# Retention: the query and key products of chunks 1 to 7 in one matmul over both parts of u and one over the upper part

## The chip, the cores and the metric

One core of a Trainium2 chip runs the whole program in one launch. The metric is the device time of one execution in microseconds (us). Engines are written as the profile writes them: PE is TensorE's matmuls, PEld its weight loads, DVE is VectorE, ACT is ScalarE, POOL is GpSimd, SP is the engine that issues the weight loads from HBM.

## The reference, cut to what matters

The reference is a transformer of six layers over 256 rows of 1024 numbers. Each layer has a mixer and an MLP; the first and the fourth mixer are retention:

```python
def retention(u, positions, w_in, decay_logit, w_out):
    q, k, v, g = jnp.split(u @ w_in, [qk, 2 * qk, 2 * qk + vd], axis=-1)
    q = rotary(split_heads(q, RET_HEADS), positions) * (RET_QK_DIM ** -0.5)
    k = rotary(split_heads(k, RET_HEADS), positions)
    ...
    o = bidirectional_scan(q, k, v, lg(0), lg(1))
    o = merge_heads(rmsnorm(o)) * jax.nn.silu(g)
    return o @ w_out
```

Queries and keys are 4 heads of 256 columns each, so `u @ w_in` has 2048 columns for q and k, 2048 for v and 2048 for g. The rotation multiplies both halves of a head by a cosine table, and the swapped halves by a sine table.

## The kernel before

Everything is float32. A product is made exact enough by splitting each operand into an upper part, rounded to a short form, and a lower part, the rest; three of the four products are summed. For u the two parts lie in `U[p, k, t, l, n]`: k is one of 8 blocks of the inner dimension, t the row half, l the part (0 upper, 1 lower), n one of 128 rows. For the weights the parts lie in `whi` and `wlo`.

**Weights.** They come in 1 MB chunks, in a fixed order. SP loads chunk i into one of 4 raw buffers. ScalarE (`hi_half`, line 1464) copies each half of it to `whi`; VectorE (`lo_half`, line 2049) subtracts to get `wlo`. `whi` and `wlo` hold two chunks each. So the upper part of half x of chunk i+2 is made only once TensorE is done with half x of chunk i: `hi_half` waits for `USED[i, x]`. VectorE's subtraction waits for that copy.

**Queries and keys.** In a retention stage, chunks 0 to 7 hold the columns of q (0 to 3) and k (4 to 7), one head to a chunk. Chunk 0 goes through `gemm_up_first` into banks 0 and 1 of the accumulator memory. Chunks 1 to 7 go through `gemm_b`: for each half (128 weight columns) and each of the 8 blocks, three matmuls of 256 columns, all summed in the same half bank, 48 matmuls a chunk. They use the banks 4 + n % 4, so four chunks in turn; chunk n waits that ScalarE has copied chunk n-4 (`QKCP`), from chunk 5 on.

**What the other engines do with them.** Each engine runs its instructions in the order in which they are written. In a retention stage, where n counts the stage's chunks and "hi" and "lo" are the two splitting steps:

- ScalarE (`act_ret`): hi of chunks 0 to 2, `raw(0)`, then for n from 2 to 8: hi of chunk n+1, `raw(n-1)`. `raw` copies a chunk's sums to `raw_q`.
- VectorE (`dve_ret`): lo of chunks 0 to 3, `tables`, `rotate(0)`, then for n from 3 to 9: lo of chunk n+1, `rotate(n-2)`. `rotate` makes four operations, lines 2276 to 2282. For chunk 0 alone it first adds the two sums (line 2274), since `gemm_up_first` leaves them apart.
- After chunk 7, TensorE goes on with the columns of v and g through `gemm_a` (line 680).

Of the kernel before, what the change touches and what calls it, by code (L numbers as in the profile page):

```python
# [11 lines left out]
ALU = mybir.AluOpType  # L12
ACT = mybir.ActivationFunctionType
# [62 lines left out]
def program(nc, d, out):  # L76
    with ExitStack() as ctx:
# [3 lines left out]
        def sem(name):  # L81
            return ctx.enter_context(nc.semaphore(name))
# [20 lines left out]
        def bank(b, n=1):  # L103
            return PS[:, b * 512:(b + n) * 512]
# [410 lines left out]
        DEC = Event(sem("s_ret_decay_exp"), heads4)  # L515
        eight = [(S, n) for S in RETS for n in range(8)]
        QKCP = Event(sem("s_ret_qk_copied"), eight)
        ROT = Event(sem("s_ret_rotated"), eight)
        RV = Event(sem("s_ret_v"), [(S, n, tt) for S in RETS for n in (0, 1) for tt in range(2)])
        RG = Event(sem("s_ret_gate"), [(S, n, tt) for S in RETS for n in (2, 3) for tt in range(2)])  # L520
# [153 lines left out]
        def pe_program(e):  # L674
# [111 lines left out]
            def gemm_b(i, b, free=(), mid=None):  # L786

                for s in range(2):
# [10 lines left out]
                            mm = e.matmul(o, a[:, k, :], U[:, k, :, part, :], start=(k == 0 and n == 0), stop=(k == 7 and n == 2))  # L799
                    mm.then_inc(USED.tick((i, s)), 1)  # L800

            def gemm_up(i, b, free):

                for ev in free:
                    e.wait_ge(*ev)
                for s in range(2):
                    e.wait_ge(*lo_cut(i, s))
                    w_h, w_l = split_half(whi, i, s), split_half(wlo, i, s)
                    o = bank(b + s).rearrange("p (t l n) -> p t l n", t=2, l=2)
                    for k in range(8):  # L810
                        if k:
                            e.matmul(o[:, :, 0, :], w_l[:, k - 1, :], U[:, k - 1, :, 0, :], start=False, stop=False)  # L812
                        if k == 7:
                            e.matmul(o[:, :, 0, :], w_l[:, k, :], U[:, k, :, 0, :], start=False, stop=False)  # L814
                        mm = e.matmul(o, w_h[:, k, :], U[:, k, :, :, :], start=(k == 0), stop=(k == 7))  # L815
                    mm.then_inc(USED.tick((i, s)), 1)
# [87 lines left out]
            def pe_ret(S):  # L904
                p, c0 = PR, first[S]
                gemm_up_first(c0, 0, (S, "in"))
                for n in range(1, 8):
                    gemm_b(c0 + n, 4 + n % 4, free=[] if n < 5 else [QKCP[S, n - 4]])
                    if n == 1:
                        rows_of_r(S, p.dg, 3)  # L910

                def scores(hh):
                    e.wait_ge(*ROT[S, 4 + hh])
                    e.wait_ge(*(RPT[S, hh - 1] if hh else ROT[S, 7]))
                    for s in range(2):
                        for k in range(2):
                            mm = e.matmul(PS[:, 4 * 512 + s * 256:4 * 512 + s * 256 + 256],  # L917
                                          p.kT[:, 2 * hh + k, s * 128:(s + 1) * 128], p.qT[:, 2 * hh + k, :],
                                          start=(k == 0), stop=(k == 1))
                    mm.then_inc(RSC.tick((S, hh)), 1)  # L920

                def values(hh):
                    e.wait_ge(*RPT[S, hh])
                    for tt in range(2):
                        if hh:
                            e.wait_ge(*RON[S, hh - 1, tt])
                        if tt == 0:
                            e.wait_ge(*RV[S, hh // 2, 1])
                        for s in range(2):
                            mm = e.matmul(bank(5 + tt), p.PT[:, hh % 2, s * 256 + tt * 128:s * 256 + tt * 128 + 128],  # L930
                                          p.v[:, s, hh * 512:(hh + 1) * 512], start=(s == 0), stop=(s == 1))
                        mm.then_inc(RAV.tick((S, hh, tt)), 1)

                def turn(hh, jj):
                    b = o_bank[hh % 2][jj]
                    if hh == 0:
                        if jj:
                            e.wait_ge(*RPT[S, 3])
                    elif hh == 1:
                        e.wait_ge(*RON[S, 3, jj])  # L940
                    else:
                        e.wait_ge(*ROL[S, hh - 2, jj])
                    for kk in range(2):
                        for tt in range(2):
                            if jj == 0 and kk == 0:
                                e.wait_ge(*RGG[S, hh, tt])
                            og = p.o[hh][tt].rearrange("p a n -> p (a n)")
                            o = b * 512 + kk * 256 + tt * 128
                            k = 2 * jj + kk
                            tr = e.transpose(PS[:, o:o + 128], og[:, k * 128:(k + 1) * 128], ident[:, :])  # L950
                    tr.then_inc(RTO.tick((S, hh, jj)), 1)

                def o_ap(hh):
                    return lambda k, tt: (p.oH[hh][:, k, tt, :], p.oL[hh][:, k, tt, :])

                def v_0(c):
                    pass

                def v_1(c):
                    if c == 1:  # L960
                        scores(0)
                    if c == 2:
                        values(0)

                def g_0(c):
                    (scores, values)[c % 2](1 + c // 2)

                def g_1(c):
                    if c == 0:
                        scores(3)  # L970
                    if c == 1:
                        values(3)
                    if c >= 2:
                        turn(0, c - 2)

                for n, after in enumerate((v_0, v_1, g_0, g_1)):
                    free = (([ROT[S, 0]], [ROPE[S]]),
                            ([RV[S, 0, 0]], [RV[S, 0, 1]]),
                            ([RV[S, 1, 0]], [RV[S, 1, 1]]),
                            ([RG[S, 2, 0]], [RG[S, 2, 1]]))[n]  # L980
                    gemm_a((S, n), c0 + 8 + 4 * n, 8, u_ap, (0, 2), free=free, after=after, entry=lambda: None)
                for hh in range(3):
                    gemm_a((S, "y"), c0 + 24 + 2 * hh, 4, o_ap(hh), (0, 2), fresh=lambda k, tt: [ROL[S, hh, k // 2]],
                           free=([RG[S, 3, 0]], [RG[S, 3, 1]]), begins=(hh == 0), ends=False,
                           after=lambda c: turn(hh + 1, c), entry=(lambda: None) if hh == 0 else None)
                gemm_last(S, o_ap(3), lambda k, tt: [ROL[S, 3, k // 2]])
# [466 lines left out]
        def act_program(e):  # L1453
# [118 lines left out]
            def act_ret(S):  # L1572
                p, c0 = PR, first[S]

                def raw(n):
                    e.wait_ge(*USED[c0 + n, 1])
                    if n >= 2:
                        e.wait_ge(*ROT[S, n - 2])
                    if n == 0:

                        a = bank(0, 2).rearrange("p (s t l n) -> p s t l n", s=2, t=2, l=2)
                        ins = e.activation(p.raw_q[:, 0, :, :].rearrange("p s (t n) -> p s t n", t=2), a[:, :, :, 1, :], ACT.Copy)
                    else:
                        ins = e.activation(p.raw_q[:, n % 2, :, :], bank(4 + n % 4).rearrange("p (a n) -> p a n", a=2), ACT.Copy)
                    ins.then_inc(QKCP.tick((S, n)), 1)

                def log_decay():
                    e.wait_ge(*s_ret_par["decay"][RETN[S]])
# [451 lines left out]
        def dve_program(e):  # L2040
# [19 lines left out]
            def own(ins):  # L2060
                ins.then_inc(dve_own.tick(), 1)

            def settle():

                e.wait_ge(*dve_own.now())
# [160 lines left out]
            def dve_ret(S):  # L2226
# [40 lines left out]
                def rotate(n):  # L2267
                    s = n % 2
                    dst = (p.qT if n < 4 else p.kT)[:, 2 * (n % 4):2 * (n % 4) + 2, :]
                    e.wait_ge(*QKCP[S, n])  # L2270
                    if n == 0:
                        a = bank(0, 2).rearrange("p (s t l n) -> p s t l n", s=2, t=2, l=2)
                        x = p.raw_q[:, 0, :, :].rearrange("p s (t n) -> p s t n", t=2)
                        own(e.tensor_tensor(x, a[:, :, :, 0, :], x, ALU.add))
                        settle()
                    own(e.tensor_tensor(dst, p.raw_q[:, s, :, :], cosb, ALU.mult))
                    if n:
                        e.wait_ge(*ROT[S, n - 1])
                    own(e.tensor_tensor(p.tb, p.raw_q[:, s, :, :], sinb, ALU.mult))
                    settle()  # L2280
                    e.tensor_tensor(dst[:, 0, :], dst[:, 0, :], p.tb[:, 1, :], ALU.subtract)
                    e.tensor_tensor(dst[:, 1, :], dst[:, 1, :], p.tb[:, 0, :], ALU.add).then_inc(ROT.tick((S, n)), 1)
# [972 lines left out]
```

## Time and profile before

| | us |
|---|---|
| three runs, median | 2210.44 |
| three runs, lowest and highest | 2209.98 and 2210.93 |
| the profiled execution, first to last instruction | 2208.3 |
| PE busy | 2174.9 |
| DVE busy | 1481.4 |
| ACT busy | 1196.9 |

Busy time of an engine is the time in which it had at least one instruction in flight. Matmuls overlap each other, so the time that one costs is read from the distance between the starts of two, not from its duration. The two retention stages begin at 0 and at about 1020 us of the profile.

### The profile page before, as it was taken

How to read it: one execution, taken by the hardware profiler on the slowest of the kernel's cores; microseconds unless marked ns; L12 is line 12 of the kernel's file. 1: busy time of each engine (PE TensorE's matmuls, PEld its weight loads, DVE VectorE, ACT ScalarE, POOL GpSimd, SP SyncE). 2: the span in 40 equal slices, each digit the busy share in tenths (PEclk: the TensorE clock that was granted, in tenths of full speed). 3: DMA queues.
4: the chain of work that ended last, by engine and by line, in shares of the span. 5: the costliest groups of instructions: out<-in, count | busy, mean ns of one | idle time of the engine just before them, and what ended most of it. 6: DMA issues, size and time to landing. Idle time of an engine off the chain costs nothing.

```text
span 2208.3 us, 29721 instructions
## 1 busy us (share of the span) xinstructions
PE 2174.9 (98%) x11776; PEld 1838.2 (83%) x11776; DVE 1481.4 (67%) x2057; ACT 1196.9 (54%) x1814; POOL 217.1 (10%) x228
## 2 busy tenths in 40 slices
PE   9999999999999999999999999999999999999999
PEld 9878888997888878888877888787888888877887
DVE  7645755897556767657745755687655699685655
ACT  5555544756445645455555544566544566475443
POOL 0000100472000011000000200002000100051000
PEclk9999999999999999999999999999999999999999
DMA  8544656524655435555544655551655566513653
GB/s 267 185 134 153 203 191 191 164 76 121 210 190 164 171 115 193 189 191 172 184 148 157 176 189 193 180 172 58 205 191 191 176 174 190 172 39 103 200 189 119
DMA packets 201817, 368.95 MB, mean 167 GB/s; under 512 B 6991, under 2 KB 142543, under 8 KB 201680
## 3 DMA queue, kind: packets, MB, share of 16 engines
q1 hardware_dynamic: 198064, 358.70, 49.7%
q0 software_dynamic: 3616, 8.35, 2.3%
q8 instruction: 95, 1.56, 0.3%
q14 instruction: 42, 0.34, 0.0%
HBM read 365.97 MB, written 1.05 MB: 166 GB/s over the span
## 4 chain that ended last, share of the span: by engine, by line
PE 90%; DVE 6%; ACT 2%; POOL 1%; issue 1%; DMA 0%; DVEq 0%; ACTq 0%; POOLq 0%
PE PS L680 48%; PE PS L815 14%; PE PS L812 6%; PE PS L799 6%; PE PS L850 2%; PE PS L1009 2%; PE PS L930 1%; DVE wlo L2049 1%; PE PS L857 1%; PE PS L1100 1%; PE PS L814 1%; POOL wlo L2977 1%; ACT whi L1464 1%; PE PS L1364 1%; PE PS L917 1%
## 5 line engine op out<-in xcount | busy, mean ns | idle before, releaser
L2049 DVE TENSOR_TENSOR wlo<-raw,whi 128x1024 fp32r<-128x1024 f32 x658 | 790.7, 1229 | 181.2 <-ACT whi L1464 180.4
L1464 ACT ACTIVATE whi<-raw 128x1024 fp32r<-128x1024 f32 x680 | 699.8, 1054 | 363.9 <-PE PS L680 309.0
L680 PE MATMUL PS<-whi,U 128*128 128x512 f32 x1728 | 483.8, 396 | 6.5 <-DVE U L2086 1.4
L815 PE MATMUL PS<-U,whi 128*128 128x512 f32 x1344 | 474.4, 397 | 0.0
L680 PEld LDWEIGHTS PS<-whi,U 128*128 128x128 f32 x1728 | 321.6, 188 | 80.8 <-issue 13.5
L812 PE MATMUL PS<-U,wlo 128*128 128x256 f32 x1176 | 330.0, 281 | 0.0
L815 PEld LDWEIGHTS PS<-U,whi 128*128 128x128 f32 x1344 | 247.1, 188 | 48.6
L2173 DVE TENSOR_TENSOR AR<-PS,AR 128x512 f32<-128x512 f32 x96 | 66.3, 691 | 309.3 <-ACT AR L1550 309.3
L680 PE MATMUL PS<-wlo,U 128*128 128x512 f32 x864 | 267.4, 391 | 0.0
L1550 ACT ACTIVATE AR<-PS 128x512 f32<-128x512 f32 x96 | 57.6, 600 | 368.6 <-PE PS L815 358.6
L680 PE MATMUL PS<-whi,fH 128*128 128x512 f32 x824 | 255.8, 392 | 0.9 <-DVE fL L2311 0.9
L680 PE MATMUL PS<-whi,fL 128*128 128x512 f32 x824 | 253.8, 389 | 0.0
L680 PE MATMUL PS<-wlo,fH 128*128 128x512 f32 x824 | 253.8, 389 | 0.0
L812 PEld LDWEIGHTS PS<-U,wlo 128*128 128x128 f32 x1176 | 222.1, 189 | 6.5
L680 PEld LDWEIGHTS PS<-wlo,U 128*128 128x128 f32 x864 | 162.5, 188 | 34.8
L2977 POOL TENSOR_TENSOR wlo<-raw,whi 128x1024 fp32r<-128x1024 f32 x22 | 52.2, 2390 | 1339.4 <-ACT whi L1464 870.3
L680 PEld LDWEIGHTS PS<-wlo,fH 128*128 128x128 f32 x824 | 154.7, 188 | 32.8
L680 PEld LDWEIGHTS PS<-whi,fL 128*128 128x128 f32 x824 | 154.7, 188 | 32.2
L680 PEld LDWEIGHTS PS<-whi,fH 128*128 128x128 f32 x824 | 153.2, 188 | 30.7 <-DVE wlo L2049 1.3
L799 PE MATMUL PS<-U,whi 128*128 128x256 f32 x768 | 139.1, 284 | 0.0
L799 PEld LDWEIGHTS PS<-U,whi 128*128 128x128 f32 x768 | 119.7, 192 | 0.4 <-DVE wlo L2049 0.3
L799 PE MATMUL PS<-U,wlo 128*128 128x256 f32 x384 | 108.6, 283 | 0.0
(342 smaller groups left out, 2356.1 us busy)
## 6 DMA issues: line engine op xcount, KB each, us to landing
raw<-in_mlp_w_up SPq DMA_DIRECT2D x64, 1024.0 KB, 5.6
raw<-in_mlp_w_down SPq DMA_DIRECT2D x64, 1024.0 KB, 5.0
raw<-in_ret_w_in SPq DMA_DIRECT2D x48, 1024.0 KB, 5.2
raw<-in_m_w_up SPq DMA_DIRECT2D x32, 1024.0 KB, 5.5
raw<-in_m_w_down SPq DMA_DIRECT2D x32, 1024.0 KB, 4.9
raw<-in_kv_w SPq DMA_DIRECT2D x24, 1024.0 KB, 5.2
raw<-in_ret_w_out SPq DMA_DIRECT2D x16, 1024.0 KB, 4.9
raw<-in_gla_w_in SPq DMA_DIRECT2D x12, 1024.0 KB, 5.1
```

The source lines that it names most:

```text
L680: mm = e.matmul(bank(b + nb), a, w[:, nb * 512:(nb + 1) * 512], start=(begins and n < 2), stop=(ends and n >= 4))
L799: mm = e.matmul(o, a[:, k, :], U[:, k, :, part, :], start=(k == 0 and n == 0), stop=(k == 7 and n == 2))
L812: e.matmul(o[:, :, 0, :], w_l[:, k - 1, :], U[:, k - 1, :, 0, :], start=False, stop=False)
L814: e.matmul(o[:, :, 0, :], w_l[:, k, :], U[:, k, :, 0, :], start=False, stop=False)
L815: mm = e.matmul(o, w_h[:, k, :], U[:, k, :, :, :], start=(k == 0), stop=(k == 7))
L850: e.matmul(o, w[:, k, :], U[:, k, tt, :, :], start=(tt == 0 and k == 0), stop=False, skip_group_check=True)
L1009: e.matmul(PS[:, b * 512 + o:b * 512 + o + 256], p.diag[:, tap_turn[c, jt] % 32, :], p.hc[:, c, jt:jt + 256], start=(jt == 0), stop=(jt == ...
L1464: e.activation(split_half(whi, i, x), raw_halves(i)[x], ACT.Copy).then_inc(HI.tick((i, x)), 1)
L1550: e.activation(m_t[f % 2].rearrange("p (s n) -> p s n", s=4), a[:, :, 1, :], ACT.Copy).then_inc(MT.tick((S, f)), 1)
L2049: e.tensor_tensor(split_half(wlo, i, x), raw_halves(i)[x], split_half(whi, i, x).bitcast(F32), ALU.subtract).then_inc(LO.tick((i, x)), 1)
L2173: e.tensor_tensor(x.rearrange("p (s n) -> p s n", s=4), a[:, :, 0, :], m_t[f % 2].rearrange("p (s n) -> p s n", s=4), ALU.add).then_inc(MX ...
L2977: e.tensor_tensor(split_half(wlo, i, x), a, split_half(whi, i, x).bitcast(F32), ALU.subtract).then_inc(LO_SEAM.tick((i, x)), 1)
```

## The change

`gemm_heads` takes the place of `gemm_b` for chunks 1 to 7 of both retention stages. For each half, 8 matmuls of 512 columns multiply the upper weights with both parts of u, into a bank whose columns are kept apart by part; then 8 matmuls of 256 columns add the product of the lower weights with the upper part of u. One half takes a bank, a chunk two: odd chunks use banks 4 and 5, even ones 6 and 7. From chunk 3 on, chunk n waits that VectorE has added the two sums of chunk n-2 (`QKADD`). TensorE waits for `HI` before a half and for the lower weights in its middle. ScalarE copies the sums of the lower part to `raw_q` and VectorE adds those of the upper part to it before it rotates, as both did before for chunk 0 alone.

```diff
+        QKADD = Event(sem("s_ret_qk_added"), eight)
+        def qk_bank(n):
+            return 0 if n == 0 else 4 if n % 2 else 6
...
+            def gemm_heads(i, b, free):
+                for ev in free:
+                    e.wait_ge(*ev)
+                for s in range(2):
+                    e.wait_ge(*HI[i, s])
+                    w_h, w_l = split_half(whi, i, s), split_half(wlo, i, s)
+                    o = bank(b + s).rearrange("p (t l n) -> p t l n", t=2, l=2)
+                    for k in range(8):
+                        e.matmul(o, w_h[:, k, :], U[:, k, :, :, :], start=(k == 0), stop=False, skip_group_check=True)
+                    e.wait_ge(*lo_cut(i, s))
+                    for k in range(8):
+                        mm = e.matmul(o[:, :, 0, :], w_l[:, k, :], U[:, k, :, 0, :], start=False, stop=(k == 7),
+                                      skip_group_check=True)
+                    mm.then_inc(USED.tick((i, s)), 1)
...
-                    gemm_b(c0 + n, 4 + n % 4, free=[] if n < 5 else [QKCP[S, n - 4]])
+                    gemm_heads(c0 + n, qk_bank(n), [QKADD[S, n - 2]] if n >= 3 else [])
...
-                    if n == 0:
-                        a = bank(0, 2).rearrange("p (s t l n) -> p s t l n", s=2, t=2, l=2)
-                        ins = e.activation(p.raw_q[:, 0, :, :].rearrange("p s (t n) -> p s t n", t=2), a[:, :, :, 1, :], ACT.Copy)
-                    else:
-                        ins = e.activation(p.raw_q[:, n % 2, :, :], bank(4 + n % 4).rearrange("p (a n) -> p a n", a=2), ACT.Copy)
-                    ins.then_inc(QKCP.tick((S, n)), 1)
+                    a = bank(qk_bank(n), 2).rearrange("p (s t l n) -> p s t l n", s=2, t=2, l=2)
+                    e.activation(p.raw_q[:, n % 2, :, :].rearrange("p s (t n) -> p s t n", t=2), a[:, :, :, 1, :],
+                                 ACT.Copy).then_inc(QKCP.tick((S, n)), 1)
...
-                    if n == 0:
-                        a = bank(0, 2).rearrange("p (s t l n) -> p s t l n", s=2, t=2, l=2)
-                        x = p.raw_q[:, 0, :, :].rearrange("p s (t n) -> p s t n", t=2)
-                        own(e.tensor_tensor(x, a[:, :, :, 0, :], x, ALU.add))
-                        settle()
+                    a = bank(qk_bank(n), 2).rearrange("p (s t l n) -> p s t l n", s=2, t=2, l=2)
+                    x = p.raw_q[:, s, :, :].rearrange("p s (t n) -> p s t n", t=2)
+                    e.tensor_tensor(x, a[:, :, :, 0, :], x, ALU.add).then_inc(QKADD.tick((S, n)), 1)
+                    e.wait_ge(*QKADD[S, n])
```

## Rows read from the trace of the kernel before

**Rows 1.** The page: busy time of TensorE, and the chain that ended last.
```profile
PE 2174.9 (98%) x11776; PEld 1838.2 (83%) x11776; DVE 1481.4 (67%) x2057; ACT 1196.9 (54%) x1814; POOL 217.1 (10%) x228
...
PE 90%; DVE 6%; ACT 2%; POOL 1%; issue 1%; DMA 0%; DVEq 0%; ACTq 0%; POOLq 0%
```

**Rows 2.** TensorE's waits (total, times, longest): the longest of all.
```profile
PE PS L1364 <- DVE AR L2873: 3.6, 5, 1.9
```

**Rows 3.** Timeline of TensorE, first stage (start, length, instructions): edges of chunks 1, 2, 8.
```profile
20.90 0.40 PE L799 MATMUL PS<-U,whi 128*128 128x256 f32 x2
...
26.66 0.60 PE L886 MATMUL PS<-AR,ones 128*128 128x128 f32 x4
27.02 0.48 PE L799 MATMUL PS<-U,whi 128*128 128x256 f32 x2
...
61.66 0.63 PE L680 MATMUL PS<-whi,U 128*128 128x512 f32 x2
...
62.59 1.07 PE L680 MATMUL PS<-whi,U 128*128 128x512 f32 x4
...
63.95 1.07 PE L680 MATMUL PS<-whi,U 128*128 128x512 f32 x4
```

**Rows 4.** Timeline of TensorE in an MLP, where 512 and 256 columns alternate.
```profile
234.17 0.40 PE L815 MATMUL PS<-U,whi 128*128 128x512 f32 x1
...
236.65 0.28 PE L814 MATMUL PS<-U,wlo 128*128 128x256 f32 x1
```

**Rows 5.** Timeline of ScalarE, first stage: the copies to `whi`, with waits.
```profile
32.96 2.01 ACT L1464 ACTIVATE whi<-raw 128x1024 fp32r<-128x1024 f32 x2 [0.50 <-DMA raw<-in_ret_w_in]
...
61.86 1.06 ACT L1464 ACTIVATE whi<-raw 128x1024 fp32r<-128x1024 f32 x1 [1.76 <-PE PS L799]
```

**Rows 6.** Timeline of VectorE, first stage.
```profile
34.12 0.69 DVE L2274 TENSOR_TENSOR AR<-PS,AR 128x512 f32<-128x512 f32 x1
34.84 0.69 DVE L2276 TENSOR_TENSOR AR<-AR 128x512 f32<-128x512 f32 x1
...
36.85 2.35 DVE L2049 TENSOR_TENSOR wlo<-raw,whi 128x1024 fp32r<-128x1024 f32 x2
39.12 0.69 DVE L2276 TENSOR_TENSOR AR<-AR 128x512 f32<-128x512 f32 x1
...
43.39 0.68 DVE L2276 TENSOR_TENSOR AR<-AR 128x512 f32<-128x512 f32 x1
...
62.96 1.23 DVE L2049 TENSOR_TENSOR wlo<-raw,whi 128x1024 fp32r<-128x1024 f32 x1 [1.40 <-ACT whi L1464]
64.10 0.69 DVE L2276 TENSOR_TENSOR AR<-AR 128x512 f32<-128x512 f32 x1
```

**Rows 7.** The chain in order of time: from VectorE's end to TensorE's start.
```profile
84.11 0.14 issue
```

**Rows 8.** Timeline of TensorE at that place.
```profile
84.24 0.70 PE L680 MATMUL PS<-whi,U 128*128 128x512 f32 x2 [0.63 <-DVE AR L2287]
```

**Rows 9.** Timeline of VectorE, second stage: lo of chunk 4, second half.
```profile
1044.91 1.23 DVE L2049 TENSOR_TENSOR wlo<-raw,whi 128x1024 fp32r<-128x1024 f32 x1 [0.33 <-ACT whi L1464]
```

**Rows 10.** Stretches: busy of PE, PEld, DVE, ACT, POOL; then granted clock, DMA.
```profile
506.00:507.00 1.00, 0.61 (x2) 0.55 (x3) 0.63 (x4) 0.89 (x3) 0.00 (x0) 0.57 0.00 0
...
508.00:509.00 1.00, 1.00 (x4) 0.80 (x3) 1.00 (x3) 0.40 (x1) 0.00 (x0) 0.50 0.00 0
509.00:510.00 1.00, 1.00 (x4) 0.73 (x3) 0.96 (x2) 0.97 (x3) 0.00 (x0) 0.72 0.00 0
```

**Rows 11.** Timeline of TensorE at that place.
```profile
506.39 1.19 PE L680 MATMUL PS<-whi,U 128*128 128x512 f32 x2 [1.11 <-DVE U L2502]
...
510.24 1.08 PE L680 MATMUL PS<-whi,U 128*128 128x512 f32 x4
```

**Rows 12.** Timeline of TensorE at another fall (1943), and the same transposes later.
```profile
1942.48 1.07 PE L1364 MATMUL PS<-AR 64*128 64x128 f32 x12 [1.86 <-DVE AR L2873]
1943.48 2.82 PE L1379 MATMUL PS<-ident,xn 128*128 128x128 f32 x12
...
1987.69 1.53 PE L1379 MATMUL PS<-ident,xn 128*128 128x128 f32 x12
```

## The prediction

> **What bounds the kernel now.** I read the page first: TensorE is busy for 98% of the span and holds 90% of the chain that ended last [rows 1]. Then its waits: the longest single one of the whole program is 1.9 us [rows 2], and none lies in the chunks that the change touches. So a microsecond of matmuls saved is a microsecond gained, and every new wait of TensorE is paid in full. Then the timelines of the three engines in the first retention stage. TensorE takes chunk 1 from 20.90 to 26.66 us, which is 48 matmuls at a pitch of 0.120, and runs on without a gap until chunk 8 starts at 61.66 [rows 3]. ScalarE and VectorE work inside that: what they do per chunk is hidden, but the order in which they do it decides what TensorE will wait for once it depends on one of them.
>
> **The matmuls.** Before, a half chunk is 24 x 0.120 = 2.88 us. After, it is 8 of 512 columns and 8 of 256. From 62.59 to 63.95 six matmuls of 512 columns start, so 0.227 each [rows 3], and 256 columns keep 0.120: 8 x 0.227 + 8 x 0.120 = 2.78 us, a gain of 0.10. The nearest row of the same mixture is that of the MLP: seven pairs in 236.65 - 234.17 = 2.48 us [rows 4], so 8 pairs in 2.83, a gain of 0.05. I take 0.10, since the new order groups the widths; the MLP's row is the lower bound and 0.11 the upper. There are 2 stages x 7 chunks x 2 halves = 28: a gain of 2.8 us (1.4 to 3.1). The columns are as many as before, and only the instructions are a third fewer.
>
> The Trainium skill, "TensorE: Matmul & The Clock Gate", section "Wait — 56ns, not 53.3ns?", gives a matmul in a row its columns at 2.4 GHz and about 2.5 ns. By that a half chunk would gain 8 x 2.5 ns = 0.02 us, the whole 0.6. The rows here show 13 ns over the columns' time both at 256 and at 512, so they disagree with it, and the sum goes by them.
>
> **What goes beside other work.** VectorE gets 14 additions (7 chunks, 2 stages); the one of chunk 0 takes 0.69 us and the next operation starts 0.72 after it [rows 6]. Where VectorE runs unbroken, from one rotation to the next is 43.39 - 39.12 = 4.3 us [rows 6]; with 0.72 it is 5.0, under the 5.56 of a new chunk. So VectorE as an amount of work still fits, and after chunk 7 its waits for ScalarE take the addition up. ScalarE's copy keeps its size. The additional waits of TensorE inside a half (`HI`, then lo) are for things done a chunk earlier: nothing.
>
> **The new wait is not hidden.** Before, four banks in turn let TensorE run four chunks ahead of ScalarE's copies. Now two pairs of banks turn, and chunk n+1 waits for the addition of chunk n-1. That addition stands in VectorE's order behind lo of chunk n+2 (the loop makes lo of chunk n+1, then `rotate(n-2)`). Lo of chunk n+2 waits for hi of chunk n+2, and the hi of its second half waits for `USED[n, 1]`, the last matmul of chunk n, since `whi` holds two chunks. So TensorE can't start chunk n+1 when chunk n ends: it waits for a full round through ScalarE and VectorE. That isn't a deadlock, as each step waits for an earlier one, but it is a stall ahead of each of the chunks 3, 4, 5, 6 and 7, in both stages: ten.
>
> Its price, step by step, from the moment at which the next matmul would have started:
> - to the start of hi: 61.86 - 61.66 = 0.20 [rows 3, 5]
> - hi to lo: 62.96 - 61.86 = 1.10 [rows 5, 6]
> - lo to the next operation of VectorE: 64.10 - 62.96 = 1.14 [rows 6]; this next one is now the addition
> - the addition: 0.69 [rows 6]
> - VectorE's end to TensorE's start: 0.14 [rows 7]
> - the first matmuls after a wait run slower: two take 0.70 [rows 8] where two take 0.63 without a wait [rows 3], 0.07.
>
> Sum 3.34 us (I allow 3.2 to 3.5). What is queued behind TensorE's wait is the whole stream of matmuls, and with it `USED`, and so the hi of the next chunks: the round can't overlap the next one.
>
> The first of the ten is longer, in the first stage. There hi of chunk 4 starts at 32.96, when its weights land [rows 5], and VectorE is behind: `rotate(0)` from 34.12, lo of chunk 4 from 36.85, next operation at 39.12 [rows 6]. None of these moves. So chunk 3 can start at 39.12 + 0.69 + 0.14 = 39.95. TensorE gets there at 20.90 + 5.56 + 0.44 (the small matmuls between, 26.66 to 27.02, and the slower one behind them, 0.08 [rows 3]) + 5.56 = 32.46. Stall 7.5, with the slow start 7.6. In the second stage lo of chunk 4 waits for ScalarE in its second half [rows 9], so that stage's first stall is an ordinary one.
>
> Sum: 9 x 3.34 + 7.6 = 37.7 us lost, 2.8 gained: +34.9.
>
> **The clock.** No row shows TensorE idle for 3.34 us amid full-width matmuls, so what its clock does then is bounded from both sides. Rows near it: at 506 us, after 1.11 us idle behind matmuls of one row, the granted clock was 0.57, then 0.50, that is 1.2 GHz in place of 2.4, and it came back within 509 to 510 [rows 10]. Ten matmuls of 512 columns took 510.24 - 506.39 = 3.85 us where ten at 0.227 take 2.27 [rows 11]: 1.6 lost. The fall around 1943 followed the 1.86 us of idle time, and 12 transposes took 2.82 us [rows 12] where the same 12 take 1.53 at full clock. The new stalls are nearly twice as long as the longest of these, but what surrounds them is denser. Lower end: nothing. Upper end: ten falls at 1.6, 16 us. I take eight falls at 1.5, 12 us, because the stall is longer than each idle time after which the clock fell here. In the touched chunks this is paid in full, since the round starts from the last matmul of a chunk.
>
> The Trainium skill's same page, section "HAM oscillation — how this bites in real kernels", tells of a kernel in which each wait between bursts put the clock back to half, and the next burst started slow, every time. By that rule all ten stalls would cost a fall.
>
> **The total.** The profiled execution's span is 2208.3, the median of the runs 2210.4, so 2.1 us lie around the span; the sum is of differences within it and leaves them as they are. 2210.4 + 34.9 + 12 = 2257.3; I predict 2257, 2.1% slower.
>
> **Rivals.**
> - The stalls come but the clock stays at 2.4 GHz, or falls only after the long one: 2210.4 + 34.9 = 2245, to 2247. For it: over the chunks TensorE stays busy for 5.56 of each 8.9 us. Against it: rows 10 and 12, with less idle time. 20%.
> - Every stall costs a fall and the matmuls gain only the lower bound: 9 x 3.45 + 7.6 = 38.7, 38.7 + 16 - 1.4 = 53 us, 2264. 15%.
> - Not slower: the round is not closed. If the addition of chunk n-1 is done before chunk n ends, TensorE never waits and only the matmuls' gain stays: 2210.4 - 2.8 = 2207.6 (2207.3 to 2209). This would decide if VectorE were to reach `rotate(n-1)` before TensorE ends chunk n, so if lo of chunk n+2 didn't need chunk n's buffer. Rows 6 speak against it: 64.10 follows the lo that waited for chunk 7's end. 3%.
> - The stalls are there but shorter, since part of the round overlaps the end of the matmuls, or because only the first stage is hit: some 20 us, 2230. 4%.
> - The forecast: ten stalls and most of them with a fall, 2250 to 2262. 58%.
>
> **How the numbers follow.** Differences under 0.2% (4.4 us) can't be told from no change here. The rival without stalls is -2.8 us, inside of that. So slower has 0.96, same 0.03, faster 0.01. The range for 8 in 10 goes from the case without falls at its lower bounds (9 x 3.25 + 7.5 - 3.1 = 33.7, 2244, less 2 for the sum's error) to the case with all of them: 2242 to 2265.
>
> **What would show it.** In the changed kernel's trace TensorE should wait for the addition of VectorE ten times, near 7.5 us once and near 3.3 nine times, at the starts of chunks 3 to 7. The chunks should start some 8.9 us apart, more where the clock fell; within a chunk at full clock the half should take 2.78. The granted clock should show 0.5 for some 3 us after most stalls. VectorE's addition should start about 1.1 us after a second-half lo. I would be wrong on the main step if TensorE shows no waits in these chunks, and on the clock if the row of granted clock stays at 1.00 in both stages.

## The result, and the profile after

The changed kernel takes 2261.03 us (median of four runs, 2259.41 to 2261.79) where the kernel before takes 2210.21: a ratio of 1.0229, 95% interval 1.0217 to 1.0241. The forecast was 2257, with a range of 2242 to 2265. The profiled execution spans 2260.0 us, 51.7 more than that of before.

The page of the changed kernel, and TensorE's longest waits (total, times, longest):

```profile
PE 2190.0 (97%) x11552; PEld 1838.0 (81%) x11552; DVE 1491.7 (66%) x2071; ACT 1196.5 (53%) x1814; POOL 217.0 (10%) x228
...
PE 88%; DVE 7%; ACT 2%; DMA 1%; POOL 1%; issue 1%; SPq 0%; DVEq 0%; ACTq 0%
```
```profile
PE PS L817 <- DVE AR L2291: 35.0, 10, 8.0
```

The first line answers to rows 1: 224 matmuls fewer, yet more busy time, because part of them ran at half clock. The second answers to rows 2. L817 is the first matmul of `gemm_heads`, L2291 the addition in `rotate`. Ten waits, five in each stage, one of them 8.0 us and the nine others 3.0.

The timeline of TensorE in the first stage (start, length, instructions; in brackets the idle time ahead and what ended it), all of chunks 1 to 3, the start of chunk 4, chunk 7, and the start of chunk 8:

```profile
22.06 2.00 PE L817 MATMUL PS<-U,whi 128*128 128x512 f32 x8
23.90 1.12 PE L820 MATMUL PS<-U,wlo 128*128 128x256 f32 x8
24.86 2.00 PE L817 MATMUL PS<-U,whi 128*128 128x512 f32 x8
26.70 1.11 PE L820 MATMUL PS<-U,wlo 128*128 128x256 f32 x8
27.65 0.60 PE L908 MATMUL PS<-AR,ones 128*128 128x128 f32 x4
28.01 2.10 PE L817 MATMUL PS<-U,whi 128*128 128x512 f32 x8
29.95 1.11 PE L820 MATMUL PS<-U,wlo 128*128 128x256 f32 x8
30.89 2.00 PE L817 MATMUL PS<-U,whi 128*128 128x512 f32 x8
32.73 1.11 PE L820 MATMUL PS<-U,wlo 128*128 128x256 f32 x8
41.82 3.78 PE L817 MATMUL PS<-U,whi 128*128 128x512 f32 x8 [7.98 <-DVE AR L2291]
45.40 1.62 PE L820 MATMUL PS<-U,wlo 128*128 128x256 f32 x8
46.86 1.99 PE L817 MATMUL PS<-U,whi 128*128 128x512 f32 x8
48.69 1.11 PE L820 MATMUL PS<-U,wlo 128*128 128x256 f32 x8
52.81 3.33 PE L817 MATMUL PS<-U,whi 128*128 128x512 f32 x8 [3.01 <-DVE AR L2291]
...
84.03 3.69 PE L817 MATMUL PS<-U,whi 128*128 128x512 f32 x8 [3.00 <-DVE AR L2291]
87.56 1.11 PE L820 MATMUL PS<-U,wlo 128*128 128x256 f32 x8
88.51 2.00 PE L817 MATMUL PS<-U,whi 128*128 128x512 f32 x8
90.35 1.11 PE L820 MATMUL PS<-U,wlo 128*128 128x256 f32 x8
91.30 0.63 PE L686 MATMUL PS<-whi,U 128*128 128x512 f32 x2
```

This answers to rows 3. A half chunk at full clock goes from 22.06 to 24.86, 2.80 us. Behind a stall the first half takes 4.48 (84.03 to 88.51), and the second one 2.79 again: the half that follows the idle stretch is slow, and only that one.

From the start of chunk 1 to that of chunk 8, the first stage took 61.66 - 20.90 = 40.76 us before and takes 91.30 - 22.06 = 69.24 now; the second stage took 40.76 and takes 63.42. That is 28.5 and 22.7 us more, 51.1 of the 51.7 together. The rest (a first stage that begins 1.2 us later, and 0.6 us less in all that follows) is of the size by which two executions of one kernel differ.

One round, in the chain that ended last (start, length, what), in the second stage:

```profile
1083.59 0.96 PE PS L820 x8
1084.55 0.02 issue
1084.58 1.06 ACT whi L1486
1085.64 0.02 issue
1085.66 1.22 DVE wlo L2067
1086.89 0.61 DVE AR L2291
1087.50 0.04 issue
1087.54 3.69 PE PS L817 x8
```

In this list a piece ends where the next one takes over, so the addition stands with less than its own 0.68 us. It can be read from top to bottom as the prediction's list: the last matmuls of a chunk, the copy to `whi` that waited for them, the subtraction, the addition, and only then the next chunk. This answers to rows 5, 6 and 7.

### The profile page after: what moved, and what is told of

Read it like the earlier page. It is cut to its first block, busy times and chain, and to the rows that moved or that the text cites. A ratio compares the mean times of both kernels' runs of the same rounds, so it can differ in the third digit from the quotient of the medians.

```text
span 2260.0 us, 29291 instructions
## 1 busy us (share of the span) xinstructions
PE 2190.0 (97%) x11552; PEld 1838.0 (81%) x11552; DVE 1491.7 (66%) x2071; ACT 1196.5 (53%) x1814; POOL 217.0 (10%) x228
## 4 chain that ended last, share of the span: by engine, by line
PE 88%; DVE 7%; ACT 2%; DMA 1%; POOL 1%; issue 1%; SPq 0%; DVEq 0%; ACTq 0%
PE PS L686 47%; PE PS L837 14%; PE PS L834 6%; PE PS L817 3%; PE PS L805 3%; PE PS L872 2%; PE PS L1031 2%; DVE wlo L2067 2%; PE PS L952 1%; DMA raw<-in_ret_w_in 1%; PE PS L820 1%; PE PS L879 1%; ACT whi L1486 1%; PE PS L1122 1%; PE PS L836 1%
## 5 line engine op out<-in xcount | busy, mean ns | idle before, releaser
L837 PE MATMUL PS<-U,whi 128*128 128x512 f32 x1344 | 474.5, 397 | 0.0
L834 PE MATMUL PS<-U,wlo 128*128 128x256 f32 x1176 | 330.0, 281 | 0.0
L837 PEld LDWEIGHTS PS<-U,whi 128*128 128x128 f32 x1344 | 247.1, 188 | 48.5
L817 PE MATMUL PS<-U,whi 128*128 128x512 f32 x224 | 72.1, 476 | 35.0 <-DVE AR L2291 35.0
L817 PEld LDWEIGHTS PS<-U,whi 128*128 128x128 f32 x224 | 49.7, 232 | 47.3 <-DVE AR L2291 37.1
L2104 DVE SCALAR_TENSOR_TENSOR U<-PS,gT,U 128x128 fp32r<-128x128 f32 x192 | 52.5, 342 | 36.6 <-ACT U L1518 36.6
```

The costliest lines, as they stand in the source:

```text
L2104: ins = e.scalar_tensor_tensor(U[:, k, tt, 1, :], PS[:, o:o + 128], gT[:, S + 1, k:k + 1], U[:, k, tt, 0, :].bitcast(F32), ALU.mult, ALU.s ...
```

## Experiments

**Only the place of the addition: e1_rotate_earlier.**

```diff
                 for n in range(3, 10):
+                    rotate(n - 2)
                     lo_of(c0 + n, 1)
-                    rotate(n - 2)
```

> The changed kernel, but VectorE rotates chunk n-2 (and so adds its two sums) one place earlier in its order: ahead of lo of chunk n+1 in place of behind it. Banks, waits and matmuls as in the changed kernel. My theory (TensorE's wait closes a round through hi and lo of a chunk whose buffer is still in use): the addition is then done some 3 us into the next chunk, so eight of the ten waits vanish; only chunk 3 still waits, some 5 us in the first stage and 1 us in the second, with one fall of the clock: 2210.2 - 2.3 + 6.3 + 2 = 2216 us. Rival (the 14 additions make VectorE too slow, or two pairs of banks are too few in any order): above 2240 us.

Measured: 2217.95 us, ratio 1.0034 (1.0021 to 1.0047). Of ten waits two are left, and they are those that the swap can't remove:

```profile
PE PS L817 <- DVE AR L2291: 5.7, 2, 5.2
```

One is of 5.2 us in the first stage, one of 0.5 in the second; in the first the clock fell, around the second it stayed at 1.00. The time is 2 us above the 2216 that was expected. With the same banks, the same 14 additions and the same matmuls, 43 of the 51 us are gone. So neither VectorE's work nor the number of banks alone makes the stalls, but that the addition stands behind a subtraction which waits for the chunk that has just ended.

**Only a third pair of banks: e2_three_pairs.** VectorE's order is that of the changed kernel.

```diff
-            return 0 if n == 0 else 4 if n % 2 else 6
+            return (0, 4, 6, 0, 4, 6, 2, 4)[n]
...
-                    gemm_heads(c0 + n, qk_bank(n), [QKADD[S, n - 2]] if n >= 3 else [])
+                    qk_free = {3: [QKADD[S, 0]], 4: [QKADD[S, 1]], 5: [QKADD[S, 2]], 6: [ROPE[S]], 7: [QKADD[S, 4]]}
+                    gemm_heads(c0 + n, qk_bank(n), qk_free.get(n, []))
...
-                    free = (([ROT[S, 0]], [ROPE[S]]),
+                    free = (([QKADD[S, 3]], [QKADD[S, 6]]),
```

> The changed kernel with VectorE's order left as it is, but a third pair of banks: chunks 1 to 7 use the pairs 4, 6, 0, 4, 6, 2, 4, so that chunk n waits for the addition of chunk n-3 (chunk 6 for the tables, which read bank 3), and the first product behind chunk 7 waits for the additions of chunks 3 and 6. My theory: with one chunk more of distance the round through hi and lo isn't closed. Left are a wait of chunk 3 in the first stage (2.5 to 3.5 us, perhaps one fall of the clock, 1.7) and about 0.6 us ahead of the second rows of chunk 8 in each stage: 2212 to 2215 us. Rival (VectorE is too slow as an amount of work): the waits move by one chunk and come back, above 2230 us.

Measured: 2214.48 us, ratio 1.0018 (1.0008 to 1.0027), with ten runs from 2212.1 to 2217.7. The profiled execution is one of the quick ones (span 2210.4). In it TensorE waits at the places that were named, and for less:

```profile
34.76 2.11 PE L817 MATMUL PS<-U,whi 128*128 128x512 f32 x8 [1.82 <-DVE AR L2292]
```
```profile
66.06 0.70 PE L686 MATMUL PS<-whi,U 128*128 128x512 f32 x2 [0.36 <-DVE AR L2292]
```

The second kind comes once in each stage. The order that closes the round at a distance of two chunks doesn't at a distance of three. Around the first wait the clock stays at 1.00 (stretches of 2 us: length, busy time of PE, PEld, DVE, ACT, POOL, then granted clock and DMA), and the half behind it takes 37.65 - 34.76 = 2.89 us:

```profile
32.00:34.00 2.00, 0.94 (x8) 0.73 (x7) 1.98 (x4) 1.47 (x3) 0.00 (x0) 1.00 1.10 349
34.00:36.00 2.00, 1.24 (x5) 1.05 (x6) 1.95 (x3) 0.89 (x1) 0.00 (x0) 1.00 1.10 348
```

So 1.8 us of idle time between full chunks cost no fall here. What makes the longer runs of this kernel longer isn't in the one trace. Their mean granted clock hints at a fall: 0.995 over the whole of the two longest (2217.4 and 2217.7 us), 0.998 in the two quickest. A longer first wait with a fall behind it would fit, as in e1; it isn't shown.

**Is it the distance of two, or who releases? e8_before_two_banks.** The kernel before the change, with two banks in turn; the release is ScalarE's copy.

```diff
-                    gemm_b(c0 + n, 4 + n % 4, free=[] if n < 5 else [QKCP[S, n - 4]])
+                    gemm_b(c0 + n, 4 + n % 2, free=[] if n < 3 else [QKCP[S, n - 2]])
...
-                        ins = e.activation(p.raw_q[:, n % 2, :, :], bank(4 + n % 4).rearrange("p (a n) -> p a n", a=2), ACT.Copy)
+                        ins = e.activation(p.raw_q[:, n % 2, :, :], bank(4 + n % 2).rearrange("p (a n) -> p a n", a=2), ACT.Copy)
```

> The kernel before the change with two banks in turn in place of four: chunk n waits for ScalarE's copy of chunk n-2. It tells whether a distance of two chunks is itself too short, or only the place of the releasing operation in VectorE's order. My theory: ScalarE's copy of chunk n-2 is done some 2 us into chunk n-1, well ahead, so there is no wait: 2210.5 us, within 0.1%. Rival (a distance of two is too short with any releaser): waits at chunks 3 to 7, 2230 us or more.

Measured: 2211.27 us, ratio 1.0003 (0.9994 to 1.0012), and in chunks 1 to 7 no wait of TensorE for a bank. One wait is there, ahead of chunk 2 of the first stage, for the lower weights, which no bank decides; ScalarE starts on the weights of chunk 2 at 26.12 us in this execution and at 24.02 in that of before, so they came later:

```profile
28.50 0.50 PE L799 MATMUL PS<-U,whi 128*128 128x256 f32 x2 [0.69 <-DVE wlo L2049]
```

The second stage takes 40.76 us from chunk 1 to chunk 8, as before. The kernel before had twice the banks that it needed. Two are enough if the release comes early in the next chunk; with the same distance, it is the release's place that decides.

**Is the slow first half the clock? e3_fill_stalls.** Matmuls of no use ahead of each wait; they add nothing to the result. The trace records each of them as two.

```diff
+                    if n >= 3:
+                        for _ in range(32 if (S, n) == (RET0, 3) else 12):
+                            e.matmul(PS[:, 2 * 512:2 * 512 + 128], ones[:, :], ones[:, :], start=True, stop=True)
                     gemm_heads(c0 + n, qk_bank(n), [QKADD[S, n - 2]] if n >= 3 else [])
```

> The changed kernel with matmuls of no use ahead of each of the ten waits: 12 of 128 columns in float32 (about 2.7 us at full clock; 32 ahead of the first one, about 7 us), into a bank that nobody uses there, so that TensorE doesn't idle. The waits themselves, their releasers and all useful work stay. My theory (each idle stretch of 3.2 us costs a fall of the clock, 1.7 us): granted clock 1.00 in both stages, the time falls by 9 x 1.7 + 2.2 = 17 us to 2244 us. Rival (the slow first half chunk comes from something else, such as both parts of u being read, or the banks): the time stays at 2261 us or rises.

Measured: 2245.05 us, ratio 1.0163 (1.0146 to 1.0180), 16.0 us less than the changed kernel, where 17 were expected. The stretches, in the same columns, of the changed kernel around one stall:

```profile
1084.00:1085.00 1.00, 0.54 (x5) 0.33 (x3) 0.17 (x1) 0.42 (x1) 0.00 (x0) 1.00 0.00 0
1085.00:1086.00 1.00, 0.00 (x0) 0.00 (x0) 0.34 (x1) 1.00 (x2) 0.00 (x0) 1.00 0.00 0
1086.00:1087.00 1.00, 0.00 (x0) 0.00 (x0) 1.00 (x2) 0.12 (x1) 0.00 (x0) 1.00 0.00 0
1087.00:1088.00 1.00, 0.46 (x1) 0.46 (x2) 0.97 (x2) 0.00 (x0) 0.00 (x0) 0.80 0.10 16
1088.00:1089.00 1.00, 1.00 (x4) 0.72 (x4) 0.97 (x3) 0.00 (x0) 0.00 (x0) 0.50 0.82 131
...
1090.00:1091.00 1.00, 1.00 (x4) 0.81 (x3) 0.00 (x0) 0.00 (x0) 0.00 (x0) 0.50 1.00 414
1091.00:1092.00 1.00, 1.00 (x9) 0.94 (x9) 0.00 (x0) 0.00 (x0) 0.00 (x0) 1.00 0.24 94
```

and with the stalls filled, the timeline of TensorE around one of them and a stretch over one:

```profile
46.73 2.84 PE L932 MATMUL PS<-ones 128*128 128x128 f32 x24
49.90 2.12 PE L817 MATMUL PS<-U,whi 128*128 128x512 f32 x8 [0.33 <-DVE AR L2294]
51.85 1.11 PE L820 MATMUL PS<-U,wlo 128*128 128x256 f32 x8
```
```profile
49.00:52.00 3.00, 2.67 (x16) 2.13 (x15) 2.90 (x6) 0.00 (x0) 0.00 (x0) 1.00 0.56 128
```

The wait still ends at the same point of the round (46.73 + 3.17 = 49.90), but the first half behind it takes 2.90 us (49.90 to 52.80), not 4.48, and the clock stays at 1.00, as it does in all of both stages. So the slow half is the clock at 1.2 GHz, and it comes from idling, not from the matmuls' form or the banks. In the stall shown TensorE had just gone back to work, at 1087.54, when the clock fell: a mean of 0.80 over 1087 to 1088 puts the fall at 1087.6, and the three stretches ahead have 1.00. The rule of the Trainium skill that the prediction named ("TensorE: Matmul & The Clock Gate", section "HAM oscillation — how this bites in real kernels"), half clock behind every wait between bursts, is what this trace shows at ten stalls of ten; the shorter waits of 1.8 us in e2 and 0.5 us in e1 were not followed by a fall.

**The matmuls' form, with the stalls: e4_old_matmul_form.**

```diff
-                    for k in range(8):
-                        e.matmul(o, w_h[:, k, :], U[:, k, :, :, :], start=(k == 0), stop=False, skip_group_check=True)
                     e.wait_ge(*lo_cut(i, s))
                     for k in range(8):
+                        e.matmul(o[:, :, 0, :], w_h[:, k, :], U[:, k, :, 0, :], start=(k == 0), stop=False, skip_group_check=True)
+                        e.matmul(o[:, :, 1, :], w_h[:, k, :], U[:, k, :, 1, :], start=False, stop=(k == 7), skip_group_check=True)
                         mm = e.matmul(o[:, :, 0, :], w_l[:, k, :], U[:, k, :, 0, :], start=False, stop=(k == 7),
```

> The changed kernel with its banks, its waits on the addition and its stalls, but each half chunk again by 24 matmuls of 256 columns (the upper weights times the upper part of u, times the lower part, the lower weights times the upper part), the two sums still apart. It prices the matmuls' form by itself. My theory: at full clock a half takes 2.88 in place of 2.80 us, at half clock both are bound by their columns, so 1.5 to 2.3 us more than the changed kernel: 2263 us, with the same ten waits. Rival (the form with 512 columns is itself what makes the stages slow): back towards 2215 us.

Measured: 2261.18 us, ratio 1.0234 (1.0219 to 1.0250). The form is not what makes the stages slow, so the rival is out. But my number for its price isn't seen either: 0.2 us more than the changed kernel, where 1.5 to 2.3 were expected. The second stage, from chunk 1 to chunk 8, is 63.47 us, against 63.42. In the first stage the first wait hides it: it is 5.9 us long here and 8.0 in the changed kernel's execution, since it depends on when the weights of the first chunks land:

```profile
PE PS L818 <- DVE AR L2291: 33.0, 10, 5.9
```

In the second stage the clock hides it. Its five slow halves take 21.29 us together here and 22.01 in the changed kernel, so they give back 0.72 of the 0.77 us that the nine quick ones cost more (0.086 each, from e7 and e5 below). At half clock the form costs nothing that can be seen: the matmuls start every 0.21 us, which is 256 columns at 1.2 GHz. And the fall came earlier against TensorE's return: in the second of these stalls the clock was at 0.50 already 0.2 us ahead of it, where the changed kernel's fell just behind it, so that less of the low clock met work. The form had to be measured without stalls.

**Both repairs: e5_order_and_pairs.**

```diff
-            return 0 if n == 0 else 4 if n % 2 else 6
+            return (0, 4, 6)[n % 3]
...
-                    gemm_heads(c0 + n, qk_bank(n), [QKADD[S, n - 2]] if n >= 3 else [])
+                    gemm_heads(c0 + n, qk_bank(n), [QKADD[S, n - 3]] if n >= 3 else [])
...
-                    free = (([ROT[S, 0]], [ROPE[S]]),
+                    free = (([QKADD[S, 6]], [ROPE[S]]),
...
-                lo_of(c0, 3)
+                lo_of(c0, 2)
                 tables()
                 rotate(0)
-                for n in range(3, 10):
+                for n in range(2, 9):
                     lo_of(c0 + n, 1)
-                    rotate(n - 2)
+                    rotate(n - 1)
+                lo_of(c0 + 9, 1)
```

> The changed kernel with both repairs: a third pair of banks (chunks 1 to 7 use the pairs 4, 6, 0 in turn, so that chunk n waits for the addition of chunk n-3), and VectorE rotates each chunk directly behind lo of the chunk two further on (lo of chunks 0 to 2, tables, rotation 0, lo 3, rotation 1, lo 4, rotation 2 and so on). My theory: TensorE never waits in chunks 3 to 7, nor ahead of chunk 8, the clock stays at 1.00, and what is left is the matmuls' gain, 28 x 0.08 = 2.3 us: 2208 us, ratio 0.999. Rival (the change has another cost that the stalls hid, such as ScalarE and VectorE now reading banks beside TensorE's writes): 2211 us or more without any wait.

Measured: 2207.47 us, ratio 0.9988 (0.9979 to 0.9997): faster than the kernel before, by 2.6 us. The stretches of the two stages:

```profile
20.00:62.00 42.00, 42.00 (x249) 37.20 (x248) 38.02 (x58) 23.95 (x32) 0.95 (x2) 1.00 0.89 294
1030.00:1072.00 42.00, 42.00 (x246) 37.11 (x245) 38.06 (x57) 20.63 (x26) 0.00 (x0) 1.00 0.60 193
```

TensorE is busy in all of both, at full clock, and never waits for the addition, while VectorE is busy for 38 of 42 us: the cover of the additions is nearly used up, but it holds. From chunk 1 to chunk 8 each stage takes 39.55 us (21.94 to 61.49 in the first), 1.21 less than before.

**The form without stalls: e7_old_form_repaired.** The kernel of e5, with the matmuls of e4.

> The kernel with both repairs (e5_order_and_pairs), but each half chunk by 24 matmuls of 256 columns, as before the change; the two sums stay apart. It prices the matmuls' form without stalls. My theory: 2.88 in place of 2.80 us a half, 2.3 us more than e5_order_and_pairs: 2210.2 us. Rival (the gain is only in how the records are modelled, not in time): the same time as e5_order_and_pairs.

Measured: 2211.20 us, ratio 1.0004 (0.9995 to 1.0013), 3.7 us more than e5. Each stage takes 40.76 us from chunk 1 to chunk 8, to the hundredth the number of the kernel before. So at full clock the form is worth 1.21 us a stage, 2.4 in all, and it is the whole of the gain that the two stages show. The other 1.3 of the 3.7 us lies outside of them and stays open; it is of the size by which two executions of one kernel differ. The additions and the third pair cost nothing in these stages.

**Grouped or alternating: e6_widths_alternating.** The kernel of e5, but in each half the two widths take turns (the last two of 256 columns stand together), and the lower weights are waited for at the head:

```diff
-                    for k in range(8):
-                        e.matmul(o, w_h[:, k, :], U[:, k, :, :, :], start=(k == 0), stop=False, skip_group_check=True)
                     e.wait_ge(*lo_cut(i, s))
                     for k in range(8):
-                        mm = e.matmul(o[:, :, 0, :], w_l[:, k, :], U[:, k, :, 0, :], start=False, stop=(k == 7),
-                                      skip_group_check=True)
+                        if k:
+                            e.matmul(o[:, :, 0, :], w_l[:, k - 1, :], U[:, k - 1, :, 0, :], start=False, stop=False)
+                        if k == 7:
+                            e.matmul(o[:, :, 0, :], w_l[:, k, :], U[:, k, :, 0, :], start=False, stop=False)
+                        mm = e.matmul(o, w_h[:, k, :], U[:, k, :, :, :], start=(k == 0), stop=(k == 7))
```

> The kernel with both repairs (e5_order_and_pairs), but in each half the matmuls of 512 and 256 columns alternate, as the MLP's do, and TensorE waits for the lower weights ahead of the half. It tells what the grouping by width is worth. By the MLP's rows a half takes 2.82 in place of 2.80 us: 28 x 0.02 = 0.6 us more than e5_order_and_pairs, which the times can hardly tell; the trace should show the pitch. If the wait for the lower weights matters, TensorE waits at chunk 3 of the first stage.

Measured: 2208.09 us, ratio 0.9991 (0.9982 to 1.0000); its interval and that of e5 overlap. In the trace the second stage takes 39.82 us from chunk 1 to 8, 0.27 more than e5's. The first takes 40.64 us, and part of that is a wait for the lower weights, at chunk 2 and not at chunk 3 as expected:

```profile
29.02 0.47 PE L822 MATMUL PS<-U,whi 128*128 128x512 f32 x1 [0.38 <-DVE wlo L2068]
```

## Why the prediction was right

**What bounds the kernel.** Right. The waits are paid in full, and so is the gain: 2.4 us less in the two stages gave 2.6 in the time (e5 against the kernel before).

**The matmuls.** 2.78 us a half were forecast, 2.80 came, so the gain is 2.4 in place of 2.8 us, within its bounds. The distance of 0.227 between matmuls of 512 columns was read where the moving operand is a weight; here it is (23.90 - 22.06) / 8 = 0.230. The figure that the prediction worked out from the Trainium skill ("TensorE: Matmul & The Clock Gate", section "Wait — 56ns, not 53.3ns?"), 0.6 us for the whole, doesn't hold here: e7 and e5 differ by 2.4 in the trace.

**What goes beside other work.** Right: VectorE is busy for 10.3 us more (1481.4 to 1491.7), 14 x 0.72 being 10.1, and e5 has every addition and not one wait of TensorE for it.

**The new wait.** Right in kind, place and number: ten waits for L2291, ahead of chunks 3 to 7 of both stages. Where the next chunk would have started at 1084.38 (1083.43 and 0.95 for the last eight), it starts at 1087.54, so 3.16 us, and the first matmuls behind a wait cost 0.11 more (2.12 behind the waits of e3, at full clock, where 2.00 is usual). That is 3.27 for the 3.34 of the sum. The small difference is in the last step: from the start of the addition to TensorE's start it took 0.73 us, and I had added 0.69 and 0.14. A duration in the profile and a release overlap, which the two rows taken from different places couldn't show. The first stall is 41.82 - 33.68 = 8.1 us where 7.5 were expected. ScalarE starts on the weights of chunk 4 when they land, here at 34.94 us and not at 32.96:

```profile
34.94 2.00 ACT L1486 ACTIVATE whi<-raw 128x1024 fp32r<-128x1024 f32 x2 [0.52 <-DMA raw<-in_ret_w_in]
```

So chunk 3 starts 1.9 us later than expected, while TensorE got there only 1.2 us later. In e4 that start was at 32.38 and the idle time 5.9 us, so much of this stall is chance. The sum of all, nine times 3.27 and once 8.25, is 37.7, as forecast to the tenth; that is luck in part, since 0.6 us too much in the nine and 0.6 too little in the first cancel.

**The clock.** The range was right and the value low. All ten stalls brought a fall, where I took eight, a value between the bounds that no row decided. Behind an ordinary stall the first half took 4.31 to 4.48 us in place of 2.79; without the slow start that is 1.4 to 1.6 us, the size that rows 11 and 12 gave. Behind the long one it was 2.1. Together 15.9 us, in place of 12; e3, without the falls, is 16.0 us shorter. That is the term that was mis-sized, and with 0.4 us for the matmuls it makes up the whole difference: 2257.3 + 3.9 + 0.4 = 2261.6, for 2261.0 measured. What I weighed against a fall, that the chunks between are dense, did not count for 3.0 us of idle time. It may count for less: in e2 the clock stayed at 1.00 through 1.82 us of idle time between full chunks, where 1.86 us among small matmuls brought a fall [rows 12]. One such pair doesn't show it. The rival with a fall at each stall, given 15%, had the count that came, and its 2264 was too high since it also took the other bounds.

**The rivals.** No stall at all, had VectorE reached the addition earlier, was put at 2207.6; e5 is that case made, at 2207.5. The stalls without a fall of the clock were put at 2245 to 2247; e3 is that case, at 2245.05.

## What to carry to other kernels

When a buffer's release moves to another engine, write down where the releasing operation stands in that engine's order and what the operation ahead of it waits for; if that wait leads back to the engine that is to be released, at the distance that the buffers give, the round trip is paid on every buffer, however idle both helpers look. Price a stall of TensorE at its length plus what the lower clock takes afterwards, here 3.3 and 1.5 us. A gain of a tenth of a microsecond per half chunk is real but needs its release made early: the same matmuls cost 2.3% with two pairs of banks and the addition in one place, 0.3% with the addition one place earlier, 0.2% with a third pair, and gained 0.1% with both.

## What had not been expected of the hardware

- A stretch of 3.0 us without matmuls between chunks of 5.6 us of full work brought half clock each of nine times, and the fall came between 0.3 us ahead of TensorE's return and 0.5 us behind it. In the stall shown it is 0.80 in the stretch in which TensorE started, then 0.50. Twelve float32 matmuls of 128 columns in each, 2.8 us of work of no use (32 in the long one), kept it at 1.00 and made the program 16 us shorter.
- Beyond its columns' time a matmul costs 13 ns at 256 columns and 17 at 512 at full clock (0.120 and 0.230 us apart), and at half clock nothing that can be seen at 256 (0.21).
- Alternating the widths took 39.82 us where grouping took 39.55 for the same 14 halves, 0.02 us a half.
